# Four large tiles placed ahead of the small constants in SBUF: an order of placement changed in a tuned two-block transformer kernel

## What is computed

```python
def first_block(x, mem, ...):                # DEPTH = 2
    for l in range(DEPTH):
        h = rms_norm(x, norm_mix[l])
        x = x + (short_conv_mixer(h, ...) if l < N_A else moba_attention(h, ...))
        x = x + mem_cross_attention(rms_norm(x, norm_mem[l]), rms_norm(mem, norm_memkv[l]), ...)
        x = x + swiglu(rms_norm(x, norm_ffn[l]), ffn_w_gu[l], ffn_w_down[l])
        ...
    return rms_norm(x, norm_final)

def second_block(x, ...):                    # DEPTH_2 = 1
    h = rms_norm_2(x, g_mix[l]) * (1.0 + sc1) + sh1
    # a gated delta rule in both directions, and a latent attention, merged by two gates
    x = x + gt1 * (merged @ w_out[l])
    h = rms_norm_2(x, g_ffn[l]) * (1.0 + sc2) + sh2
    x = x + gt2 * expert_choice_ffn(h, w_router[l], w_gate[l], w_up[l], w_down[l])   # 16 experts
    return rms_norm_2(x, g_final)
```

## The kernel before

| tile | bytes | offset before | offset after |
|---|---|---|---|
| `ident`, `ones`, `vcol`, `small`, `neg_half`, `eps`, `swap1`, `swap2`, `rope1`, `rope2` | 7,360 | 98,304 | 131,072 |
| `x` | 8,192 | 105,664 | 98,304 |
| `h_hi` | 8,192 | 113,856 | 106,496 |
| `h_lo` | 8,192 | 122,048 | 114,688 |
| `xn` | 8,192 | 130,240 | 122,880 |
| `a_hi` | 22,528 | 138,432 | 138,432 |
| `F0` (scratch) | | 183,520 | 183,520 |

## Time and profile before

### The profile page before, as it was taken

One profiled execution on the slowest core, in us unless ns is written; L12 is line 12 of the kernel. 1 busy time (PEld: TensorE's weight loads), 2 busy tenths in 40 slices (PEclk: granted clock), 3 DMA queues, 4 the chain that ended last, 5 costly groups with the idle time before them and its releaser, 6 DMA issues.

```text
span 1998.1 us, 34891 instructions
## 1 busy us (share of the span) xinstructions
PE 1646.2 (82%) x14751; PEld 1336.0 (67%) x14751; DVE 881.2 (44%) x1179; ACT 661.6 (33%) x825; POOL 161.9 (8%) x195
## 2 busy tenths in 40 slices
PE   5999999999989999997978877689677666677564
PEld 5999799889869889887956777488664222222221
DVE  3764466555555466544564578644651000000002
ACT  4535455344335355433535532233332000000000
POOL 7400000000000000000030013051100000000000
PEclk8999999999989999997978988889898667576787
DMA  5765566746416567552421332012259999999995
GB/s 190 239 204 178 166 172 186 274 168 242 158 65 235 181 174 196 173 190 82 138 72 55 107 102 70 1 45 95 90 211 382 409 409 409 409 409 408 409 408 236
DMA packets 274339, 417.01 MB, mean 209 GB/s; under 512 B 12914, under 2 KB 210969, under 8 KB 274201
## 3 DMA queue, kind: packets, MB, share of 16 engines
q1 hardware_dynamic: 272112, 410.49, 58.3%
q10 hardware_dynamic: 2089, 4.49, 0.7%
HBM read 413.90 MB, written 1.05 MB: 208 GB/s over the span
## 4 chain that ended last, share of the span: by engine, by line
issue 72%; PE 16%; DVE 5%; POOL 4%; ACT 3%; DVEq 0%; POOLq 0%; ACTq 0%
PE bank L1541 3%; DVE cy L1169 2%; PE bank L359 1%; PE bank L360 1%; PE bank L361 1%; PE bank L376 1%; POOL ang L765 1%; PE bank L378 1%; PE bank L377 1%; POOL ang L764 1%; PE bank L1459 1%; ACT w_hi L239 1%; DVE w_lo L246 1%; PE bank L1665 0%; PE bank L1651 0%
## 5 line engine op out<-in xcount | busy, mean ns | idle before, releaser
L246 DVE TENSOR_TENSOR w_lo<-w_raw,w_hi 128x2048 fp32r<-128x2048 f32 (+2 forms) x179 | 403.7, 2257 | 277.1 <-ACT w_hi L239 276.8
L359 PE MATMUL bank<-h_hi,w_hi 128*128 128x256 f32 x1328 | 376.4, 283 | 12.3 <-DVE h_lo L529 10.4
L239 ACT ACTIVATE w_hi<-w_raw 128x2048 fp32r<-128x2048 f32 (+2 forms) x179 | 334.1, 1870 | 154.7 <-DMA w_raw<-in_ffn_w_down_dram 56.6
L360 PE MATMUL bank<-h_lo,w_hi 128*128 128x256 f32 x1328 | 373.4, 281 | 0.0
L361 PE MATMUL bank<-h_hi,w_lo 128*128 128x256 f32 x1328 | 373.1, 281 | 0.0
L359 PEld LDWEIGHTS bank<-h_hi,w_hi 128*128 128x128 f32 x1328 | 254.4, 192 | 16.3 <-issue 13.3
L360 PEld LDWEIGHTS bank<-h_lo,w_hi 128*128 128x128 f32 x1328 | 255.6, 192 | 0.0
L361 PEld LDWEIGHTS bank<-h_hi,w_lo 128*128 128x128 f32 x1328 | 254.0, 191 | 0.0
L376 PE MATMUL bank<-w_hi,a_hi 128*128 128x256 f32 x512 | 144.7, 283 | 0.0
L2101 DVE TENSOR_TENSOR hx<-sg,bank 128x256 f32<-128x256 f32 x16 | 6.7, 421 | 311.5 <-ACT sg L2065 311.5
L377 PE MATMUL bank<-w_lo,a_hi 128*128 128x256 f32 x512 | 143.5, 280 | 0.0
(11 more groups left out here) (444 smaller groups left out, 2830.2 us busy)
## 6 DMA issues: line engine op xcount, KB each, us to landing
w_raw<-in_ffn_w_gu_dram SPq DMA_DIRECT2D x88, 512.0 KB, 4.9
w_exp_e<-in_w_gate_dram SPq DMA_DIRECT2D x36, 1024.0 KB, 18.6
w_exp_e<-in_w_up_dram SPq DMA_DIRECT2D x32, 1024.0 KB, 18.8
w_exp_e<-in_w_down_dram SPq DMA_DIRECT2D x28, 1024.0 KB, 18.7
w_raw<-in_w_in_dram SPq DMA_DIRECT2D x54, 512.0 KB, 4.6
w_mod<-in_w_mod_dram SPq DMA_DIRECT2D x24, 1024.0 KB, 7.5
w_raw<-in_ffn_w_down_dram SPq DMA_DIRECT2D x44, 512.0 KB, 4.2
w_expw_hi<-in_w_down_dram SPq DMA_DIRECT2D x20, 1024.0 KB, 18.5
```

Source lines behind the costliest of these rows:

```text
L239: e.activation(whi[slot][:, 0:w], raw[slot][:, 0:w], ACT.Copy).then_inc(S["hi_ready"], 1)
L246: e.tensor_tensor(wlo[slot][:, 0:w], raw[slot][:, 0:w], whi[slot][:, 0:w].bitcast(F32), ALU.subtract).then_inc(S["lo_ready"], 1)
L359: e.matmul(dst, whi[slot][:, lo:hi_], bh[:, k, :], start=(k == 0), stop=False)
L360: e.matmul(dst, whi[slot][:, lo:hi_], bl[:, k, :], start=False, stop=False)
```

## The change

Four `place` calls, for `x`, `h_hi`, `h_lo` and `xn`, move from behind the ten small constant tiles to ahead of them. Sizes, types and shapes stay, and so do all instructions and their order, semaphores and transfers; what differs is the address in SBUF that an instruction holds for one of these fourteen tiles or for a tile laid over one of them.

```diff
     side = [place(f"w_mod{s}", [P, 2, D], F32) for s in range(RING)]
+    x = place("x", [P, TT, D], F32)
+    h_hi = place("h_hi", [P, KT, SEQ], F32R)
+    h_lo = place("h_lo", [P, KT, SEQ], F32R)
+    xn = place("xn", [P, TT, D], F32)
     ident = place("ident", [P, P], F32)
     ones = place("ones", [P, P], F32)
     vcol = place("vcol", [P, 256], F32)
...
     rope1 = place("rope1", [ROT, 2, SEQ], F32)
     rope2 = place("rope2", [ROPE_2, 2, SEQ], F32)
-    x = place("x", [P, TT, D], F32)
-    h_hi = place("h_hi", [P, KT, SEQ], F32R)
-    h_lo = place("h_lo", [P, KT, SEQ], F32R)
-    xn = place("xn", [P, TT, D], F32)
 
     a_hi = place("a_hi", [P, FT, SEQ], F32R)
```

## The result

In twenty runs of each, the kernel after has a median of 2008.53 us (2002.77 to 2024.32) and the kernel before one of 1998.18 us (1988.54 to 2007.59). These medians differ by 10.35 us, and 2008.53 lies beyond the upper end of the range, 2007. The ratio, taken over all fast runs (31 of the kernel after), is 1.0063, 95% interval 1.0046 to 1.0081: slower by 0.63%, about 12.6 us, where no change was forecast. The profiled execution after took 2007.96 us, its span is 2006.2 us, 8.1 us over before.

A forecast was written before the change was run, and what follows sets the result against it. It took matmuls to bound the first half, dependent steps the middle and the weight stream the experts. Terms of 0 + 0 + 0 on 1999.81 us gave 1999.8 us, no change (0.80), range 1993 to 2007.

The forecast's parts named there:

- What bounds the kernel: Whole kernel: matmuls bound the first half, dependent delta-rule steps the middle, the weight stream the experts at 398 GB/s.
- the dense matmuls: Some 5070 matmuls, mostly in fm_chunk and tm_chunk: 0 ns change each, plus or minus 5 us in all.
- the gather: Experts' rows, 16 matmuls of 512 columns with both operands at one phase: minimum 387 ns against 388, taken as no cost.
- its bound of 1 ns: Dense matmuls: plus or minus 1 ns each, from 387 against 388 ns, so plus or minus 5 us.
- the transposes: Transposes against ident: said to keep their phase, since 32,768 is four times 8192; nothing put on them.
- The first rival: fm_chunk and tm_chunk: the new phase costs, 4 ns on 5070 matmuls, 20 us slower, 2020 us; chance 0.07.
- its two mechanisms: fm_chunk and tm_chunk: both matmul operands collide, or a matmul and the next chunk's split on other engines; 20 us.
- its test: Lines L359 to L361: means with h_hi go up and those with a_hi do not.
- Its price of 4 ns on 5070 matmuls: Dense matmuls: largest difference any address pair shows, 287 against 283 ns, making 20 us.
- VectorE, ScalarE and the transfers: Some 200 operations on moved tiles, x's load and the result's store: 0, within 1 us and 0.6 us.
- The descriptor rule: Load of x and result store: off-boundary descriptors could cost some 0.6 us; both placements are off, so difference 0.
- The scatter: Whole run: clock comes out otherwise, time near 2007 with no cause in the change; chance 0.08.

The follow-up runs named there:

- the bench: TensorE alone, without the model's computation, repeating fm_chunk's matmul order at chosen operand shifts; 192 matmuls took 24.1 us at shift 0, 22.9 at 192.
- e2_x_only: Against the kernel before: only x and xn moved directly behind the weight ring, h_hi and h_lo keeping their old offset; ratio 1.0036 (1.0013 to 1.0058).
- e11_h192_a192: The change's order with swap1, neg_half, eps between ring and x, so h and a stand at 192 modulo 256; against the kernel before, 1.0022 (1.0000 to 1.0044).
- e8_before_again: The kernel before itself, unchanged, run for a second trace; this one run took 1994.50 us.
- c1_h192_a64: Against the kernel before: tiles reordered so h stands at 192 and a at 64 past a multiple of 256 from the ring; ratio 1.0005 (0.9984 to 1.0027).
- m1_phase_map: TensorE alone, fm_chunk's order, stretches of 48 matmuls at many operand shifts; mean step 119.9 ns at shift 0, 113.3 at 192.
- m2_roles: TensorE alone: 24 pauses at shift 192, the stationary operand shifted, 512 columns, spaced tiles; 18 stretches at 113.3 to 113.5 ns, 6 at 117.8.
- e7_h32_a320: Against the kernel before: constants placed so h stands 32 and a 320 bytes past the ring's period; ratio 1.0037 (1.0015 to 1.0059).

## Why the prediction was wrong, point by point

**What bounds the kernel** was read rightly: the loss arose where TensorE is full, and part of it was given back where it is not.

**The step that failed** is in the dense matmuls: "I take 0 ns each, the value of the row nearest to the new situation (387 against 388)". That row, the gather, has 512 moving columns. `Sa` and `h_hi` did stand at relation 0 in it, but the bench shows that at 512 columns the relation 0 is the shortest step of those tried (227 ns), while at 256 columns it is among the longest (120 against 113). The nearest row in address was not near in shape, and 4944 of the matmuls at stake have 256 columns. What the runs showed in place of the 0 and of its bound of 1 ns: the mean step of `fm_chunk` on h is 120.1 ns after, against 115.2 and 116.7 in the two traces of before, so 3.5 to 5 ns on each of these matmuls. After the change the gather itself stands at relation 192, and its mean step went from 227.8 to 233.4 ns (the steps under 300), where the bench has 227 and 233.

Three smaller faults stand beside it. The bound of 1 ns came from durations, which overlap. How little a duration says shows in the down projection, which did not move: L909's median went from 388 to 394 ns while the mean step stayed at 229 ns. The steps, which can be read off the same trace, showed 113 and 118 ns for one form at the full clock, and that alone said that something about these matmuls was unexplained. The medians "276 and 279" for the two roles were not one price at two phases: the roles stand at relations 192 and 64, neither at 0, and both values are drawn. And the transposes did not keep their relation: `xn` against `ident` went from 192 to 0. That cost nothing, L510 has durations of 270/273/448 ns in both traces.

**The first rival** was what happened: its place (`fm_chunk` and `tm_chunk`), its sign, the first of its two mechanisms (both operands of a matmul) and its test (rows on `h_hi` up, rows on `a_hi` not). The period of 8192 was too coarse, it is 256. Its price of 4 ns on 5070 matmuls, 20 us, is what TensorE's busy time shows (19.6 us), and that is luck: the 4 ns were the difference between 287 and 283 ns of two groups at the same relation of 64, so they were no price of an address. The second mechanism, the split on other engines, falls by the bench, where no other engine works. The end shows less, 8.1 us in this pair of executions and 1.0063, about 12.6 us, over all. Added up from the start times, the stretches on h grew by 20.0 us, those on a shrank by 1.8 (a draw), and all that lies between these stretches shrank by 7.5 us. That makes the 10.7 us by which the last `tm_chunk` stretch ends late, and the experts took 2.6 of them. The 7.5 us were not divided further: in the middle part TensorE isn't the bound, and where the clock fell in attention it fell at other times than before (0.89 and 0.94 from 540 to 600 us).

**VectorE, ScalarE and the transfers** cost nothing, as said: 1057 against 1058 ns, and 4.8, 5.0 and 4.0 us against 5.2, 4.9 and 4.0. The descriptor rule of the Trainium skill's page "DMA: Bandwidth & Descriptors" isn't tested by these runs, since both placements of `x` are off a 256-byte boundary.

**Another rule of the Trainium skill speaks of this case.** The Trainium skill's page "SBUF — State Buffer", section "Who interferes with whom", gives TensorE two read ports, one for the moving operand and one for the weight load, independent, and says that TensorE never waits on anyone. On other engines the traces agree: at relation 0 the step is 120 ns with them at work (after) and without them (the bench). On the independence of the two reads they disagree, and the measurement decides: shifting the moving operand alone makes 6 ns a matmul (24.1 against 22.9 us for 192).

**The scatter** was put down to clock or chance. The drawn step adds to it, a stretch of 1056 matmuls being worth 5 us, but it isn't the main part. In the kernel after the steps on h are not drawn, and its twenty runs lie 21.6 us apart, those of before 19.1 us. What makes the rest wasn't tested.

**Open.** What inside TensorE makes 256 the period and 192 the best relation; what fixes the draw; and whether e2_x_only (1.0036) and e11_h192_a192 (1.0022) carry a small cost of their own. In e2's trace the clock fell in the attention, 0.68 from 1060 to 1085 us against 1.00 in e8_before_again's, and the pause before the next stretch is 4.6 us longer for it. That doesn't settle it: the traces of c1_h192_a64 and e11_h192_a192 have 0.66 in the same window and the same longer pause, and took 1991.05 and 1992.34 us. One trace can't account for the median of twelve runs either. VectorE's and ScalarE's busy times in e2's trace, the same as before, give no sign of a cost of moving x and xn.

## What to carry to other kernels

Where TensorE is the bound with short float32r matmuls, the address of the moving operand minus that of the weights, modulo 256, is a parameter, worth 0.6 to 1.2% in this kernel: give it a value on purpose (192 for 256 columns here, and neither a multiple of 256 nor 96), and keep it when tiles are reordered. The kernel before already had a good one, and no placement tried was faster than it. Measure such an effect by the step from start to start in a stretch that runs without a break, not by durations. And a row that is to bound an unseen cost must be near in the shape of the operation, not only in the property that changes.

## What the runs showed of the hardware that was not expected

- At the full clock, the steps of float32r matmuls of 128 by 128 by 256 on TensorE alone follow the relation of the two operands' addresses modulo 256, the best at 113.3 ns (192) and the worst at 120.0 (0 and 96); of 512 columns, at 227 to 233 ns, in another order (m1_phase_map and m2_roles).
- At relation 192 there are two stable steps, 113 and 118 ns. Which one holds is set near the start of a stretch (18 and 6 of 24 stretches in m2_roles) and lasts, in the kernel, for a stretch of 1056 matmuls (1045 steps of 118 in the first trace of before).
- At other relations the steps repeat a fixed cycle within a stretch, such as 113, 116, 118, 120 ns at 32 (e7_h32_a320 and some stretches of m1_phase_map).
- A cost of 6 ns a matmul shows as 2 ns in the minimum of the durations (276 against 278 ns) and plainly in the counts per window (532 against 503 in 60 us).
